# A hybrid decoder layer: the first transfers, the first weight piece's low part and the place of the input rows and their squares, reordered

## The reference, cut to what matters

```python
def rmsnorm(x, g):
    xf = x.astype(jnp.float32)
    y = xf * lax.rsqrt(jnp.mean(xf * xf, axis=-1, keepdims=True) + EPS)
    return (y * g.astype(jnp.float32)).astype(x.dtype)

h = rmsnorm(x, mix_norm_gain) @ w_in            # (256, 2048) @ (2048, 5376)
qa, ka, va, qr, kr, vr, gr = jnp.split(h, splits, axis=-1)
qa = rope(qa, positions)                        # sines and cosines of positions * inv_freq
```

## Time and profile before

| | |
|---|---|
| median of 3 runs | 1934.89 us (1934.36 to 1935.78) |
| the profiled execution's own time | 1939.21 us |
| its span in the profile | 1937.4 us |
| TensorE busy | 99% of the span |
| VectorE, ScalarE, GpSimd busy | 71%, 49%, 73% |
| moved from and to memory | 450.64 MB, mean 233 GB/s |

### The profile page before, as it was taken

The page is one execution under the profiler, slowest core; times in us unless marked ns, Lnnn a source line. Parts: engine busy times, 40 slices in busy tenths (PEclk is TensorE's granted clock), DMA queues, the critical chain, the costliest instruction groups (busy, mean ns, idle before and its releaser), DMA issues.

```text
span 1937.4 us, 35319 instructions
## 1 busy us (share of the span) xinstructions
PE 1912.3 (99%) x11858; PEld 1767.6 (91%) x11858; DVE 1375.3 (71%) x2562; ACT 954.3 (49%) x1339; POOL 1410.9 (73%) x714
## 2 busy tenths in 40 slices
PE   8999999999999999999999999999999999999997
PEld 6888889887999999999999999989999999999997
DVE  6544684046445777868888888368888877999996
ACT  6453355374544444544444444444555554555555
POOL 7866768886898999988888888975555415775621
PEclk9999999999999999999999999999999999999999
DMA  9644546664665666666666666689999988999984
GB/s 334 186 142 151 198 149 221 193 194 145 216 188 181 207 207 208 207 196 195 195 194 195 192 191 193 205 303 308 337 333 332 325 270 278 345 325 334 332 259 142
DMA packets 126683, 450.64 MB, mean 233 GB/s; under 512 B 16528, under 2 KB 17424, under 8 KB 125712
## 3 DMA queue, kind: packets, MB, share of 16 engines
q1 hardware_dynamic: 101520, 365.19, 58.1%
q0 software_dynamic: 20480, 67.13, 9.9%
q10 hardware_dynamic: 4608, 17.34, 2.5%
HBM read 445.39 MB, written 4.19 MB: 232 GB/s over the span
## 4 chain that ended last, share of the span: by engine, by line
PE 55%; POOL 31%; issue 13%; DVE 1%; POOLq 0%; ACT 0%; DVEq 0%; ACTq 0%
POOL wlo L426 31%; PE ps L1864 21%; PE ps L1769 13%; PE ps L1867 11%; PE ps L1772 7%; PE ps L1783 1%; PE ps L1845 1%; PE ps L1875 0%; POOLq L425 0%; DVE wlo L1357 0%; PE ps L1847 0%; PE ps L1953 0%; DVE gate_parts L1359 0%; POOLq L429 0%; DVE x_back L1390 0%
## 5 line engine op out<-in xcount | busy, mean ns | idle before, releaser
L426 POOL TENSOR_TENSOR wlo<-raw,whi 128x1024 fp32r<-128x1024 f32 x444 | 1077.5, 2432 | 200.3 <-ACT whi L514 186.2
L514 ACT ACTIVATE whi<-raw 128x1024 fp32r<-128x1024 f32 x436 | 462.3, 1061 | 631.7 <-PE ps L1772 357.4
L1769 PE MATMUL ps<-x_parts,whi 128*128 128x448 f32 x2048 | 589.2, 369 | 1.4 <-POOL wlo L426 1.4
L1864 PE MATMUL ps<-gate_parts,whi 128*128 128x448 f32 x1992 | 581.0, 373 | 2.2 <-DVE gate_parts L1359 2.1
L686 ACT ACTIVATE whi<-raw 128x1024 fp32r<-128x1024 f32 x256 | 272.8, 1065 | 311.0 <-PE ps L1867 271.0
L1772 PEld LDWEIGHTS ps<-x_parts,wlo 128*128 128x128 f32 x2048 | 384.7, 188 | 31.4
L1867 PEld LDWEIGHTS ps<-gate_parts,wlo 128*128 128x128 f32 x1992 | 374.9, 188 | 34.3
L1772 PE MATMUL ps<-x_parts,wlo 128*128 128x224 f32 x2048 | 387.1, 270 | 0.0
L1867 PE MATMUL ps<-gate_parts,wlo 128*128 128x224 f32 x1992 | 375.8, 269 | 0.0
L1357 DVE TENSOR_TENSOR wlo<-raw,whi 128x1024 fp32r<-128x1024 f32 x248 | 304.0, 1226 | 92.1 <-ACT whi L686 68.9
L1769 PEld LDWEIGHTS ps<-x_parts,whi 128*128 128x128 f32 x2048 | 310.3, 191 | 1.7 <-ACT big L640 1.1
(11 more groups left out here) (252 smaller groups left out, 2221.3 us busy)
## 6 DMA issues: line engine op xcount, KB each, us to landing
raw<-in_w_u SPq DMA_DIRECT2D x256, 512.0 KB
raw<-in_w_v SPq DMA_DIRECT2D x256, 512.0 KB
raw<-in_w_front SPq DMA_DIRECT2D x180, 512.0 KB
big<-in_x_t ACTq DMA_DIRECT2D x4, 512.0 KB, 9.4
big<-in_x ACTq DMA_DIRECT2D x4, 512.0 KB, 7.5
big<-in_mem ACTq DMA_DIRECT2D x4, 512.0 KB, 6.9
big<-in_mem_t ACTq DMA_DIRECT2D x2, 1024.0 KB, 6.5
big<-in_x ACTq DMA_DIRECT2D x2, 1024.0 KB, 7.2
```

What stands on the lines that cost most here:

```text
L426: nc.gpsimd.tensor_tensor(wlo[:, j % SPL, :], raw[:, j % RAW, :], whi[:, j % SPL, :], ALU.subtract).then_inc(lo_done, 1)
L514: nc.scalar.activation(whi[:, j % SPL, :], raw[:, j % RAW, :], ACT.Copy).then_inc(hi_done, 1)
L1769: nc.tensor.matmul(sums[:, 0:2 * TD], whi[:, s, cols], x_parts[:, :, m, 0:TD], start=m == 0, stop=False, skip_group_check=True)
L1864: nc.tensor.matmul(sums[:, 0:2 * TD], whi[:, s, cols], gate_parts[:, g].rearrange("p k t -> p (k t)"), start=False, stop=False, skip_group ...
```

## The change

The turned input comes in five chunks of 2, 2, 4, 4 and 4 instead of four of 4, and is issued by SyncE between the first four pieces, chunk 0 first. ScalarE issues only the gains, and then runs a tiny copy of WARM, so that its table is loaded there. ScalarE splits pair 0 of the input before piece 0, and piece 0 in two halves. The low part of piece 0 moves from GpSimd to VectorE, also in halves, behind pair 0; GpSimd's first body of twelve pieces is written out from piece 1 on. TensorE may start piece 0 on its first half. The input rows' DMAs move from behind pieces 2 to 5 to behind 5 to 8, the memory rows' from 7 to 10 to 8 to 11, the squares of x from 6 and 7 to 9 and 10, the root from 9 to 11. The sines stay at 13.

```diff
+X_CHUNKS = [slice(0, 2), slice(2, 4), slice(4, 8), slice(8, 12), slice(12, 16)]
...
             for j in range(RAW):
+                m = X_CHUNKS[j]
+                sp.dma_start(XT[:, m, :], x_t[:, m, :]).then_inc(xT_in[j], 16)
                 sp.dma_start(raw[:, j, :], w_front[j]).then_inc(raw_in[j], 16)
+            sp.dma_start(XT[:, X_CHUNKS[RAW], :], x_t[:, X_CHUNKS[RAW], :]).then_inc(xT_in[RAW], 16)
...
-            with pool.Fori(0, POOL_END // BODY) as i:
+            pool.wait_ge(lo_done, 1)
+            for j in range(1, BODY):
+                rest_of(0, j)
+            with pool.Fori(1, POOL_END // BODY) as i:
                 for j in range(BODY):
                     rest_of(i * BODY, j)
...
             act.dma_start(GAIN, gain_cols.rearrange("p (a b) -> p a b", a=6)).then_inc(gain_in, 16)
-            for q in range(4):
-                act.dma_start(XT[:, 4 * q:4 * q + 4, :], x_t[:, 4 * q:4 * q + 4, :]).then_inc(xT_in[q], 16)
+            act.wait_ge(warm_ready, 1)
+            nc.scalar.activation(stats[:, UNREAD:UNREAD + 1], WARM[:, 0:1], ACT.Copy)
...
-                    act.wait_ge(xT_in[b // 2], 16)
+                    act.wait_ge(xT_in[b if b < 2 else b // 2 + 1], 16)
...
+            split_high(A_X, 0)
+            act.wait_ge(raw_in[0], 16)
+            nc.scalar.activation(whi[:, 0, 0:PW // 2], raw[:, 0, 0:PW // 2], ACT.Copy).then_inc(hi_half, 1)
+            nc.scalar.activation(whi[:, 0, PW // 2:], raw[:, 0, PW // 2:], ACT.Copy).then_inc(hi_done, 1)
             for j in range(U0):
-                high(j)
+                if j:
+                    high(j)
...
             dve.wait_ge(gain_in, 16)
-            for b in range(8):
+            split_low(A_X, 0)
+            for part, ready, done in ((slice(0, PW // 2), hi_half, lo_half), (slice(PW // 2, PW), hi_done, lo_done)):
+                dve.wait_ge(ready, 1)
+                nc.vector.tensor_tensor(wlo[:, 0, part], raw[:, 0, part], whi[:, 0, part], ALU.subtract).then_inc(done, 1)
+            for b in range(1, 8):
                 split_low(A_X, b)
...
-                pe.wait_ge(lo_done, n + 1)
+                if n:
+                    pe.wait_ge(lo_done, n + 1)
+                else:
+                    pe.wait_ge(lo_half, 1)
                 s = n % SPL
                 for tb in range(TB):
                     for c in range(PW // width):
+                        if n == 0 and tb == 0 and c == 1:
+                            pe.wait_ge(lo_done, 1)
...
-for _b in range(8):
+for _b in range(1, 8):
     _act(_b // 2, ("x", _b))
 for _b in range(4):
-    _act(2 + _b, ("load_rows", _b))
-    _act(7 + _b, ("load_memory_rows", _b))
-for _n, _s in ((6, ("load_ident", 0)), (6, ("square_x", 0)), (7, ("square_x", 1)), (9, ("root_x", 0)),
+    _act(5 + _b, ("load_rows", _b))
+    _act(8 + _b, ("load_memory_rows", _b))
+for _n, _s in ((6, ("load_ident", 0)), (9, ("square_x", 0)), (10, ("square_x", 1)), (11, ("root_x", 0)),
```

More of the change, by code:

```diff
@@ L318, in hymba_layer @@
         x_in, mem_in = [sem(f"x_in{i}") for i in range(TB)], [sem(f"mem_in{i}") for i in range(TB)]
-        xT_in, memT_in = [sem(f"xT_in{i}") for i in range(4)], [sem(f"memT_in{i}") for i in range(2)]
+        xT_in, memT_in = [sem(f"xT_in{i}") for i in range(5)], [sem(f"memT_in{i}") for i in range(2)]
+        hi_half, lo_half = sem("hi_half"), sem("lo_half")
         const_in, keys_in = sem("const_in"), sem("keys_in")
```

## The result

The changed kernel is slower: 1938.38 us median of 18 runs against 1935.54 for the kernel before in 18 runs beside it, ratio 1.0018 with a 95% interval of 1.0011 to 1.0025. The medians differ by 2.84 us, where I had forecast -0.6 and a range up to 1937.2, which is +2.3. The ratio and its interval are a figure of their own and not the quotient of the two medians, which would be 1.0015.

The account below looks back on a forecast made before the run. The prediction took TensorE, busy 99% of the span, as the bound. Start -2.5 us, given back +1.9 at VectorE's chain, made -0.6: 1934.89 - 0.6 = 1934.3 us, range 1931.0 to 1937.2.

Parts of the forecast that it names:

- The start: TensorE's first real product: at about 7.2 us instead of 9.68, a gain of 2.5 us.
- the carried term: Low clock at TensorE's start: carried as before, ten products at 0.43 us.
- Pieces 1 to 12: Weight pieces behind the start: splits and loads hidden by 1.7 us of slack a piece, so the earlier start is kept.
- The squares: ScalarE's squares of x: last row landing by 33.4, variances starting at 35.1 to 35.5, 5.3 to 5.7 us later.
- rival 3: Sines' wait takes more than the start gave: rows land at 34.4, P(20), piece 20's start, +2.3, 1937.2; chance 0.15.
- the angle chain: VectorE, variances to angles: taken at 9.2 us, giving back 1.9 us of the start's gain at piece 20.
- rival 1: Angle chain runs undelayed on VectorE: angles at 43.1, P(20), piece 20's start, -1.8, 1933.1; chance 0.17.
- The piece 12 term: Piece 12's weights: land at 36 to 37, wanted at 37.1, so the split's DMA wait goes.
- The luck term: Low-level products after TensorE's idle gap near 1297: a shifted start can lose or repeat them, up to 2 us either way.
- rival 2: The start's gain is kept whole: -2.4 to -5 us, 1932.0 as the middle; chance 0.20.

Follow-up runs that it names:

- the kernel with VectorE's low parts: Changed kernel with the low parts of pieces 1 to 7 also on VectorE, GpSimd starting at piece 8; ratio 1.0000 to the kernel before.
- late rows and squares only: Kernel before with only the rows, squares and root moved as in the change; 2.52 us slower than the kernel before, ratio 1.0016.
- new start only: Changed kernel with rows, memory rows, squares and root at their old places; +0.17 us against the kernel before, ratio 1.0001.
- Angles first: Changed kernel with VectorE's variances behind the angles instead of ahead of them; +1.28 us against the kernel before, ratio 1.0007.
- the last kernel of the table: Changed kernel with rows, squares, root at old places, low parts to piece 7 on VectorE, sines behind 12; -2.43 us against the kernel before, ratio 0.9990.
- the input row ahead of the memory row: Changed kernel with the last input row's DMA issued ahead of the first memory row's behind piece 8; +3.90 us against the kernel before, ratio 1.0016.
- the rows early and the squares late: Changed kernel with input and memory rows issued at their old places, squares and root still late; -0.31 us against the kernel before, ratio 1.0000.

## Why the prediction was wrong

**The start: right.** Forecast 7.2, measured 7.25; the gains' landing, 4.58, set it (4.64 forecast), and the table load was out of the way at 2.48. The low clock took 0.33 us more up to piece 1 than the carried term.

**Pieces 1 to 12: the first failure.** I called every cover there good and left one step out, VectorE's low parts of pairs 2 to 7. In the changed kernel twelve of them take 18.97 us. TensorE, 2.1 us earlier, meets them at piece 5 and waits 1.4, and again briefly at piece 6: of the start's gain 0.20 is left at piece 6 and 0.06 at piece 7. These instructions read two SBUF operands, and while GpSimd works five of the twelve take 0.47 us and seven 1.6 to 2.7; in the kernel with VectorE's low parts, where GpSimd is idle at that time, two take 0.88 together. The rule of the Trainium skill that I cited for the angles ("SBUF — State Buffer", Who interferes with whom) agrees with this trace, and it bore on the term that I hadn't written down. How many of the twelve are stretched differs from profile to profile: six in the kernel before (17.15 us in all) and eight with late rows and squares only (21.40), where TensorE waits for them with the old start too. With the new start only they take 18.90, and TensorE doesn't wait.

**The squares: the step that failed.** "The last of them goes out with the split of piece 8, at 26.2, and 7.2 as before gives 33.4; a shorter queue gives less." It went out at 28.72 and took 9.7, to 38.4. Of those 5.0 us, 2.5 is the late issue and 2.5 the landing. The issue is late by the waits at pieces 5 and 6 and the low clock (without the waits, in the kernel with VectorE's low parts, it is at 26.12, and the landing again 9.7). The queue was not shorter: the list puts the first memory row in front of the last input row, and from 26 to 40 us the DMA engines moved 393 to 415 GB/s. So the sign of that argument was wrong, and it was the one by which I called rival 3 less likely. That the row landed in 3.4 us when it went ahead of the memory row doesn't show what the order is worth, as told at that kernel.

**Two ways to piece 20, not one.** I let the angle chain carry the whole price. It was shorter than thought, 7.4 us from 40.45 to 47.85 instead of 9.2: GpSimd stood still until 41.58, and the first instruction and the pair took 0.17 and 0.52 instead of 0.85 and 2.70, as rival 1 had it. But ScalarE's stand also held the split of piece 11. My text checks only piece 12's; by its own count piece 11's would start at 35.1 and be wanted by 36.0. With a start at 40.45 it costs 2.0 at P(11). Angles first shows the split: 1.3 of 2.6 remain.

**Rival 3 came true** in its mechanism and, by luck, in its price. It had 0.15, and +2.3 for a landing at 34.4. The landing was 4.0 later than that; the chain was 2.9 shorter than the 10.3 it was priced with, and VectorE's list from the first tile to the second's end took 20.8 instead of 21.7. These errors cancel, and +2.63 is left at piece 20.

**The piece 12 term** was right in nothing but the missing wait. I had its weights landing at 36 to 37. Its load in SyncE's timeline, and the landing time of that load:

```profile
32.06 0.35 SPq L384 DMA_DIRECT2D raw<-in_w_front  x1
```

```profile
raw<-in_w_front SPq DMA_DIRECT2D x1, 512.0 KB, 8.7
```

It goes out only behind the low part of piece 8, which I hadn't counted, and lands at 40.8. The wait is absent because ScalarE itself reached that split late, behind square 1.

**The luck term** exists, and it was too small: the gap near 1296 is in the profile of before and not in that of after, and it cost 4.3 us there (0.4 just ahead of it, 2.2 in the gap, 1.7 in the products at the low level behind it), where I had allowed up to 2. Of the other ten profiles one has it, that of the last kernel of the table. It isn't what the medians' difference shows, which follows P(20) within 1 us in seven of the eleven kernels; the largest exception, 2.4, is the input row ahead of the memory row. In rival 2 the middle of 1929.9 to 1932.5 is 1931.2 and not 1932.0; nothing hangs on it.

## What to carry to other kernels

When a change starts one engine earlier, list every producer that this engine meets in the following pieces and ask for the rate of each, not only for the weights' chain; the slowest one takes the gain back within a few pieces. A transfer moved behind a step is issued when that step runs, so any wait of the step moves it, and what stood ahead of it on its queue landed first in every pair read here: write issue and landing as a chain with its own slack. A step that waits for such a transfer in a hand-ordered list holds all that is listed behind it.

## What the runs showed of the hardware that I had not expected

The landing of one equal 512 KB transfer, the last input row's, ranged from 3.4 to 9.7 us. It took 9.0 to 9.7 in the four profiles in which it went out 0.36 us behind a memory row, and 3.4 in the one in which it went out ahead of it and the DMA engines moved 256 GB/s instead of 411. Order and load changed together, and which of them did it isn't shown.

TensorE's low level at the start isn't of one length. The kernel before had it for 10 products from 9.68 and the changed one for 13 from 7.25. The new start alone began at the high level, waited 1.92 for piece 1, and then dropped to the low one, as its timeline shows:

```profile
11.99 0.47 PE L1505 MATMUL ps<-whi,x_parts 128*128 128x512 f32 x1 [1.92 <-POOL wlo L431]
...
12.78 0.63 PE L1505 MATMUL ps<-whi,x_parts 128*128 128x512 f32 x1
```

So among the five profiles with the start of the changed kernel piece 2 begins anywhere from 14.66 to 16.41. The level can also fall later. With the input row ahead of the memory row it fell behind a wait of 1.96 at piece 4, and the clock granted from 24 to 26 us was 0.53; behind waits of 2.03 and 2.02 at the same piece, with the rows early and the squares late and with the angles first, it didn't fall:

```profile
22.50 0.80 PE L1505 MATMUL ps<-whi,x_parts 128*128 128x512 f32 x1 [1.96 <-DVE x_parts L822]
23.09 0.63 PE L1506 MATMUL ps<-wlo,x_parts 128*128 128x512 f32 x1
```

That this is part of why the medians scatter around the shift of P(20) is likely but not shown.
